# The last heads of a DeltaNet layer and of an attention layer: out-projection in half units at other places, output split on its own semaphore, weight halves earlier, and the mask multiply behind the block solve

## The reference

```python
def gated_deltanet(x, w_in, conv_w, a_log, dt_bias, norm_w, w_out):
    h = x @ w_in
    ...
    qkv = jax.nn.silu(causal_dwconv(qkv, conv_w))
    ...
    o = gated_delta_rule_chunked(q, k, v, g, beta).astype(x.dtype)
    o = rms_norm(o, norm_w) * jax.nn.silu(gate.reshape(B, T, GDN_HEADS, GDN_DV))
    return o.reshape(B, T, GDN_V) @ w_out
...
    low = jnp.where(strict, jnp.einsum('nbhid,nbhjd->nbhij', kb, k) * decay, 0.0)
    a_mat = low + jnp.eye(C, dtype=f32)
    sol = lax.linalg.triangular_solve(a_mat, rhs, left_side=True, lower=True, unit_diagonal=True)
    attn_intra = jnp.where(causal, jnp.einsum('nbhid,nbhjd->nbhij', q, k) * decay, 0.0)
...
def diff_attention(...):
    ...
        p = jax.nn.softmax(s, axis=-1)
        p = p[:, :, 0] - lam * p[:, :, 1]
        return jnp.einsum('bhqk,bkhe->bqhe', p.astype(v.dtype), v)
    ...
    o = rms_norm(o, subln_w) * (1.0 - lambda_init)
    return o.reshape(B, T, D_MODEL) @ w_out
```

## Time and profile before

| | |
|---|---|
| median of 3 runs | 1480.03 us (1477.89 to 1480.41) |
| profiled execution: own time, span | 1480.16 us, 1478.4 us |
| TensorE busy | 1419.7 us, 96% of the span |
| DVE, ACT, POOL busy | 868.4, 627.6, 81.2 us |
| mean granted TensorE clock | 0.991 |

### The profile page before, as it was taken

The page is one execution under the profiler, slowest core; times in us unless marked ns, Lnnn a source line. Parts: engine busy times, 40 slices in busy tenths (PEclk is TensorE's granted clock), DMA queues, the critical chain, the costliest instruction groups (busy, mean ns, idle before and its releaser), DMA issues.

```text
span 1478.4 us, 20384 instructions
## 1 busy us (share of the span) xinstructions
PE 1419.7 (96%) x7138; PEld 1159.2 (78%) x7138; DVE 868.4 (59%) x1369; ACT 627.6 (42%) x1001; POOL 81.2 (5%) x92
## 2 busy tenths in 40 slices
PE   8999999999899999999999899999899999999997
PEld 7778887788778888887888686677688888887886
DVE  4666676656657666666423527777585666664225
ACT  4565455654433444444221235656524444443121
POOL 3000000000000000000001001111000000000002
PEclk9999999999999999999999999999999999999999
DMA  6212211121112333333332131112221333333321
GB/s 187 65 50 65 57 46 39 50 64 58 46 36 62 99 99 99 99 98 126 114 100 72 57 88 55 43 57 75 97 71 58 100 99 93 96 115 122 100 89 68
DMA packets 157724, 118.82 MB, mean 80 GB/s; under 512 B 5898, under 2 KB 145644, under 8 KB 157676
## 3 DMA queue, kind: packets, MB, share of 16 engines
q1 hardware_dynamic: 157676, 118.17, 26.4%
HBM read 116.04 MB, written 2.11 MB: 80 GB/s over the span
## 4 chain that ended last, share of the span: by engine, by line
PE 85%; DVE 9%; ACT 3%; issue 2%; DMA 1%; DVEq 0%; SPq 0%; ACTq 0%
PE bank L1524 15%; PE bank L1526 15%; PE bank L1525 15%; PE bank L1512 8%; PE bank L1513 8%; PE bank L1514 8%; PE bank L1579 3%; PE bank L1586 2%; PE bank L1878 1%; PE bank L1896 1%; DVE w_lo L342 1%; PE bank L1837 1%; ACT w_hi L337 1%; DVE Tc L1051 1%; DVE scr L1020 1%
## 5 line engine op out<-in xcount | busy, mean ns | idle before, releaser
L1524 PE MATMUL bank<-x_hi,w_hi 128*128 128x512 f32 (+1 forms) x1160 | 458.7, 395 | 6.5 <-DVE acc_a L1344 3.5
L1526 PE MATMUL bank<-x_hi,w_lo 128*128 128x512 f32 (+1 forms) x1160 | 438.2, 378 | 0.0
L1525 PE MATMUL bank<-x_lo,w_hi 128*128 128x512 f32 (+1 forms) x1160 | 438.0, 378 | 0.0
L342 DVE TENSOR_TENSOR w_lo<-raw,w_hi 128x1024 fp32r<-128x1024 f32 x196 | 240.1, 1227 | 274.1 <-ACT w_hi L337 268.7
L337 ACT ACTIVATE w_hi<-raw 128x1024 fp32r<-128x1024 f32 x188 | 196.2, 1050 | 189.2 <-PE bank L1514 157.8
L1524 PEld LDWEIGHTS bank<-x_hi,w_hi 128*128 128x128 f32 x1160 | 219.7, 189 | 45.9 <-issue 4.2
L1526 PEld LDWEIGHTS bank<-x_hi,w_lo 128*128 128x128 f32 x1160 | 219.1, 189 | 41.0
L1525 PEld LDWEIGHTS bank<-x_lo,w_hi 128*128 128x128 f32 x1160 | 219.8, 189 | 37.3 <-issue 3.3
L1512 PE MATMUL bank<-w_hi,u_hi 128*128 128x512 f32 x416 | 166.0, 399 | 10.8 <-issue 5.7
L1513 PE MATMUL bank<-w_lo,u_hi 128*128 128x512 f32 x416 | 163.8, 394 | 0.0
L1514 PE MATMUL bank<-w_hi,u_lo 128*128 128x512 f32 x416 | 163.7, 394 | 0.0
(11 more groups left out here) (278 smaller groups left out, 1787.9 us busy)
## 6 DMA issues: line engine op xcount, KB each, us to landing
raw<-in_ffn_w_up SPq DMA_DIRECT2D x88, 512.0 KB, 3.7
raw<-in_ffn_w_down SPq DMA_DIRECT2D x44, 512.0 KB, 3.3
raw<-in_gdn_w_in SPq DMA_DIRECT2D x32, 512.0 KB, 4.2
raw<-in_diff_w_in SPq DMA_DIRECT2D x24, 512.0 KB, 3.7
raw<-in_gdn_w_out SPq DMA_DIRECT2D x8, 512.0 KB, 3.3
raw<-in_diff_w_out SPq DMA_DIRECT2D x8, 512.0 KB, 3.2
x_tok<-in_x SPq DMA_DIRECT2D x4, 512.0 KB, 5.6
ROW<-decay_rows SPq DMA_DIRECT2D x8, 256.0 KB, 3.2
```

What stands on the lines that cost most here:

```text
L342: nc.vector.tensor_tensor(w_lo[:, s, :], raw[:, (base + r) % RAW, :], w_hi[:, s, :].bitcast(F32), ALU.subtract).then_inc(lo_ready, 1)
L1524: nc.tensor.matmul(out, hi, x_hi[:, k, cols], start=(k == 0), stop=False)
L1525: nc.tensor.matmul(out, hi, x_lo[:, k, cols], start=False, stop=False)
L1526: ins = nc.tensor.matmul(out, lo, x_hi[:, k, cols], start=False, stop=last)
```

## The change

1. **GDN_FILL and ATT_FILL.** The fillings of both last heads go by half units: an entry is (place, tb, half, k), three matmuls. The first ones of the DeltaNet head write only bank 0, the wait for bank 1 stands at the first half unit that writes it. The DeltaNet head gets 30 half units (three of them of `tb` 2) where it had 28; the attention head 24, as before, at other places.
2. **Own semaphores.** The four output instructions count on `o_dve`; ACT's differences on `diff_act`. In the last DeltaNet head `gated(6)` (`o1`, `og`) stays ahead of `L` on DVE, and `halves_out(6)` (`hi`, `lo`) goes behind `RV`.
3. **differences(7)** (eight small ACT instructions, L680) goes from the start of head 7 into head 6, ahead of the k tap. ACT's loop covers heads 1 to 4, and heads 5 and 6 are written out.
4. **Held weights.** `hold_hi` and `hold_lo` of out-projection chunk 4 go earlier; chunks 5 to 7 wait on `o_dve`.
5. **Mask order.** In every DeltaNet head `A` goes behind `T0`; TensorE waits for it ahead of transposing `TM`.
6. **Attention weights.** An extra split of q/k chunk 3 stands ahead of attention head 0 (on DVE between `rope(0, 0)` and `rope(0, 1)`), and every head splits chunks `2h + 4` and `2h + 5` in place of `2h + 3` and `2h + 4`.

```diff
-ATT_FILL = [(1, 0, 0), (7, 0, 1), (8, 0, 2), (9, 0, 3), (10, 1, 0), (11, 1, 1), (12, 1, 2), (13, 1, 3), (14, 0, 4),
+GDN_FILL = [(0, 0, 0, 0), (1, 0, 0, 1), (2, 0, 0, 2), (3, 1, 1, 0), (4, 1, 1, 1), (5, 1, 1, 2), (6, 0, 1, 0), (7, 0, 1, 1),
+ATT_FILL = [(0, 0, 0, 0), (1, 0, 0, 1), (2, 0, 1, 0), (3, 0, 1, 1), (5, 0, 0, 2), (6, 0, 1, 2), (7, 0, 0, 3),
...
@@ ACT, DeltaNet step @@
+                if more and not first:
+                    differences(h, e)
                 if not first:
-                    differences(h, e)
                     decays(h, e)
...
+                if not more:
+                    hold_hi(act, C_GDN_OUT + WS, (d_dve, D_DVE0 + h * DVE_N))
...
-                    for k in range(WS, HEADS):
-                        hold_hi(act, C_GDN_OUT + k, (d_dve, D_DVE0 + h * DVE_N))
+                    for k in range(WS + 1, HEADS):
+                        hold_hi(act, C_GDN_OUT + k, (o_dve, O_N * h))
...
+                    if isinstance(h, int) and h == HEADS - 2:
+                        differences(h + 1, 1 - e)
                     tap(h + 1, 2)
@@ ACT, attention step @@
-                split_hi(act, C_QK, it, 2 * r + 3)
+                split_hi(act, C_QK, it, 2 * r + 4)
                 if not more:
-                    split_hi(act, C_QK, it, 2 * r + 4)
+                    split_hi(act, C_QK, it, 2 * r + 5)
...
             take(0, 1)
+            split_hi(act, C_QK, 0, 3)
             step(0, 0)
@@ DVE, DeltaNet step @@
+                if not more:
+                    gated(h - 1, 1 - e)
                 pe("kk")
                 act("DD")
...
-                pe("qk")
-                act("DT")
-                nc.vector.tensor_tensor(AT[e][:, :, :], v3(X(e, 1)), DT[e][:, :, :], ALU.mult).then_inc(d_dve, 1)
                 if not more:
                     split_lo(dve, C_GDN_IN, h, 7)
                 solve(h, e)
...
+                pe("qk")
+                act("DT")
+                nc.vector.tensor_tensor(AT[e][:, :, :], v3(X(e, 1)), DT[e][:, :, :], ALU.mult).then_inc(d_dve, 1)
                 pe("kt")
...
                 masked(0)
+                if not more:
+                    hold_lo(dve, C_GDN_OUT + 4)
...
                 if not more:
-                    hold_lo(dve, C_GDN_OUT + 4)
+                    halves_out(h - 1, 1 - e)
@@ DVE, attention @@
             rope(0, 0)
+            split_lo(dve, C_QK, 0, 3)
             step(0, 0)
@@ TensorE @@
-            def unit(i, tb, k, c, K, hi, lo, held, done):
+            def unit(i, tb, k, c, K, hi, lo, held, done, which=BOTH):
...
-                for half in range(2):
+                for half in which:
...
+                        for tb, half, k in [piece for p, *piece in GDN_FILL if p0 <= p < p1]:
+                            if (tb, k) == (0, 0):
+                                pe.wait_ge(bank_read[half], T_UP[0] // 2 + 1)
...
+                            mixer_unit(0, tb, k, (half,))
...
                     if i == 0:
+                        dve("A")
                         four(1, at(TM), None, turn=True)
...
-            for k in range(HELD):
-                mixer_unit(0, 2, k)
-            pe.wait_ge(d_dve, D_DVE0 + HEADS * DVE_N)
+            mixer_unit(0, 1, HEADS - 2, (1,))
+            for k in range(3):
+                mixer_unit(0, 2, k, (1,))
+            mixer_unit(0, 2, 3)
+            mixer_unit(0, 2, 4)
+            pe.wait_ge(o_dve, O_N * HEADS)
```

91 lines of the change are left out of this document (46 added, 45 removed), and 7 rows, old and new, of tables (ATT_FILL, GDN_FILL).

## The result

The changed kernel takes 1470.99 us (median of 4 runs, 1469.95 to 1472.1) where the kernel before, on the same chip, takes 1480.22 us (median of 4, 1477.89 to 1482.4). The ratio is 0.9936, 95% interval 0.9922 to 0.9951: 9.2 us less. The profiled execution took 1472.10 us, with a span of 1470.3 us, 8.1 less than the span of before.

What follows compares the result with a forecast made beforehand. TensorE, busy for 96% of the span, was taken as the bound, with only idle and low-clock time to win. Terms -3.8 - 6.3 + 1.4 - 1.9 + 1.6 = -9.0 us gave 1471.0 us, range 1467.0 to 1475.5.

Steps and rivals of the forecast that it cites:

- The mask order: DeltaNet heads 0 to 6: mA behind T0 shortens the second solve step, T0 0.54 us earlier per head; 3.8 us gained.
- The last DeltaNet head: Last DeltaNet head: earlier kk and T0, less idling up to and behind ms; 6.3 us gained, bounds 4.5 and 7.5.
- Attention head 0: Attention head 0: DVE's extra split on the path to the first scores; 1.4 us lost, bounds 1.1 to 1.7.
- The last attention head: Last attention head: chunk 3 wait goes, new 3.0 us wait at k 2; 1.9 us gained, bounds 0.5 and 3.
- The clock: TensorE's clock falling behind new long waits: 1.6 us lost, bounds 0 and 3.3.
- one drop: Clock step: the new 3.0 us wait probably brings a drop, the 1.8 us wait probably not; 1.6 us charged.
- The sum: Whole kernel: all terms together give 9.0 us less, 1471.0 us.
- the fourth row: Stretch from the first FFN's first up tile to attention head 0's first scores: 1.4 us predicted lost.
- only the last heads gain: Rival, DeltaNet heads 0 to 6: second solve step stays long or POOL collides elsewhere; 1474.8 us, chance 0.10.
- the wait moves to `kk`: Rival, start of last DeltaNet head: late k norm keeps the 2.3 us wait and clock loss; 1474.9 us, chance 0.09.
- The slower rival: Rival, all eight DeltaNet heads: moved A and mA locking out a DVE split count in full; 1490.1 us, chance 0.03.
- The two clock rivals: Rivals: both new waits drop the clock, 1472.7 us, or neither does, 1469.4 us; chance 0.19 together.

Runs made afterwards that it cites:

- e1: Kernel before with only the mask order changed: A behind T0 on DVE in all eight heads, so mA later on POOL; 1474.56 us, ratio 0.9956.
- e2: Kernel before with one POOL edit: mA waits for T0 in place of A, DVE's order untouched; 1475.00 us, ratio 0.9965.
- e8: Changed kernel with two half units of k 3 moved ahead of T0 in the last DeltaNet head; 1471.74 us, ratio to before 0.9945.
- e11: Changed kernel with the last DeltaNet head's first half units in whole-unit order, banks 0 and 1 alternating; 1470.90 us, ratio to before 0.9940.
- e10: Changed kernel with ACT's differences of the last DeltaNet head back in that head's own step; 1471.02 us, ratio to before 0.9935.
- e3: Changed kernel with attention head 0's extra weight split moved behind the first maxima, ahead of the first mix; 1468.91 us, ratio to before 0.9925.
- e4: Changed kernel with the last attention head's first two k 2 half units moved from ahead of turn(1) to behind values(1); 1467.27 us, ratio to before 0.9905.
- e9: Changed kernel with POOL's mA held until KD is done, so it begins where DVE's weight split does; 1470.38 us, ratio to before 0.9936.
- e12: Changed kernel with attention head 0's split behind the first maxima, k 2 half units behind values(1), POOL's QD behind T0; 1463.22 us, ratio to before 0.9883.

## Why the prediction was right, point by point

**The mask order, 3.8 us.** Right in mechanism and size: 3.81 us in the trace, the same in e1, and e2 shows that it is `mA`'s place alone. That the stretched step delays `T0` one for one, and that TensorE's wait takes all of it, holds too: with the idle times under 0.15 us counted, the seven waits fell from 4.9 to 1.1 us, by the 3.8 that the heads gained. The cover named for `A` (0.65 us of DVE's idle time ahead of `PB`) was enough.

**The last DeltaNet head, 6.3 us.** 6.7 measured. `kk` came 5.75 us after `ms`, where the prediction has 5.8. The new wait for `T0` is 1.57 us, 1.8 were predicted; and e8 shows that it can't be filled from behind. From `ms` to `ms` 5.6 us were gained, 4.9 predicted: the idle times that I found level by level were too long, 0.84 us in all from 382.48 to 411.39 in place of 2.0. Behind `ms` 1.1 us were gained, 1.4 predicted. Starting with three half units on bank 0 is worth 1.5 us by e11; that a drop of the clock can go with the wait at bank 1 was seen only at the 2.3 us of the kernels with the old start. The early differences, which I counted as needed, are worth 0.4 (e10), and `A` and `mA` behind the solve 1.15 (e1). The own semaphore, the later `halves_out` and the earlier held weights weren't taken apart: what each is worth isn't shown.

**Attention head 0, 1.4 us lost.** 1.6 by e3, within the bounds, and above the value taken because the copy of `vh` did hold the split up: 1.62 us in place of 1.22.

**The last attention head, 1.9 us gained.** The mechanism was right to the tenth: 3.0 us predicted at the first half unit of `k` 2, 3.02 measured. In all 1.0 us was gained there in spite of a drop of the clock of 1.3 (e4), so the term without the clock measured 2.3 us where 1.9 was taken (bounds 0.5 and 3).

**The clock, 1.6 us lost.** This term was mis-sized: 3.4 us in the profiled execution, just over the bound of 3.3. The price of a drop was right (1.6 us), and at the two new waits it went as predicted: the drop in the attention layer came (1.3), and none came at `T0`. But a further 1.6 us were lost behind the untouched wait at 465.95, and 0.5 because two old low stretches no longer began inside a wait; the prediction has neither. The step that failed is "one drop", as if drops hung on the waits that the change touches. They don't: see the section on the hardware. The larger gains in the two last heads made up for part of it.

**The sum.** 9.0 us predicted, 9.2 by the medians and 8.1 by the spans. The median of 1470.99 us against the 1471.0 predicted is luck in its last digits: the kernel's own four executions lie 2.2 us apart, and by the stretches the forecast has a loss 2.3 us too small in the fourth row, and gains 0.4, 0.7 and 0.3 us too small in three others. **The rivals.** That only the last heads gain is excluded by e1 and e2. That the wait moves to `kk` is excluded by the trace: ACT did the differences in its gap. The slower rival had a price that was too high: it let `mA` lock a split out for its whole 1.30 us. In e9 the split starts first and loses nothing, and in e12, with `mA` 0.6 us ahead of it, it loses 0.54 us. The two clock rivals, a drop at both new waits or at neither, didn't come in the profiled execution of the changed kernel; in e8 one came behind the 1.70 us wait of attention head 0, for which the prediction has none.

## What to carry to other kernels

A short dependent chain on DVE should be read against POOL's timeline, not only its own: one elementwise POOL instruction for which no engine waited cost every head 0.54 us, and one changed wait value on POOL brought it back without touching DVE. When half units or other filler wait for data of their own, put them behind whatever on the same engine could run in that wait: e4 won 3.4 us by moving two tuples behind three groups that were ready, 1.3 of them because no low clock followed. And where a kernel is at 97% of its bound, compare stretches between common marks instead of totals, since single executions differ by whole drops of the clock.
